# A mixed order for the heads, the rotary and the attention of a hybrid encoder on one core

## The reference

```python
proj = rmsnorm(h, norm_mix_even) @ w_in_ab            # z, x/B/C, dt, q, k, v: 24 tiles of 128 columns
# state space, 8 heads of 64, 2 groups, both directions
y = (d_skip[0] + d_skip[1]) * xs
for direction in range(2):
    dt = softplus(dt_raw + dt_bias[direction]);  A = -exp(a_log[direction])
    y = y + ssd_direction(xs, dt, A, bm, cm, reverse=(direction == 1))
ssd_out = rmsnorm_by_group(y * silu(z), norm_w)
# differential attention, 4 heads, two maps of 64 channels each, values of 128
q, k = partial_rotary(q), partial_rotary(k)
p = softmax(q @ k.T * 64 ** -0.5)
o = (p[:, :, 0] - lam * p[:, :, 1]) @ v
attn_out = rmsnorm(o, subln_w) * (1 - lambda_init)
h = h + concatenate([ssd_out, attn_out]) @ w_out_ab
h = h + swiglu(rmsnorm(h), w_gate, w_up, w_down)      # layer 0's second half
```

## Time and profile before

| what | us |
|---|---|
| median of 3 runs | 1687.55 |
| lowest and highest | 1683.24, 1688.83 |
| the profiled execution | 1691.67 |
| its span, first to last instruction | 1689.6 |
| its mean granted TensorE clock | 0.970 |

### The profile page before, as it was taken

One profiled execution on the slowest core, in us unless ns is written; L12 is line 12 of the kernel. 1 busy time (PEld: TensorE's weight loads), 2 busy tenths in 40 slices (PEclk: granted clock), 3 DMA queues, 4 the chain that ended last, 5 costly groups with the idle time before them and its releaser, 6 DMA issues.

```text
span 1689.6 us, 22187 instructions
## 1 busy us (share of the span) xinstructions
PE 1646.3 (97%) x8386; PEld 1365.2 (81%) x8390; DVE 1257.0 (74%) x1206; ACT 987.6 (58%) x905; POOL 65.1 (4%) x79
## 2 busy tenths in 40 slices
PE   8999899999999998999999999999999999999997
PEld 7766389999869667788888888888888888888886
DVE  5275766665456454788988988988988988988984
ACT  3363444443256412677777777776776777777673
POOL 0141000000100410000000000000000000000000
PEclk9989899999979897999999999999999999999998
DMA  8322035567305321899999999999999999999991
GB/s 273 100 75 75 1 100 175 174 202 221 100 17 167 116 85 65 300 373 342 355 372 340 359 368 342 358 367 344 357 368 346 352 371 342 356 371 343 354 370 74
DMA packets 221109, 429.55 MB, mean 254 GB/s; under 512 B 9506, under 2 KB 76584, under 8 KB 220736
## 3 DMA queue, kind: packets, MB, share of 16 engines
q1 hardware_dynamic: 217816, 424.82, 70.8%
q10 hardware_dynamic: 3240, 4.03, 0.7%
HBM read 427.77 MB, written 1.05 MB: 254 GB/s over the span
## 4 chain that ended last, share of the span: by engine, by line
PE 91%; DVE 4%; ACT 3%; issue 1%; DMA 1%; ACTq 0%; DVEq 0%
PE ps L1557 89%; PE ps L1574 3%; ACT arena L702 1%; DVE arena L999 0%; DVE ring_lo L1174 0%; DVE sq L1155 0%; ACT arena L601 0%; DMA raw<-in_moe_w_gate_dram 0%; DMA ktab<-in_k_table_dram 0%; DVE arena L1120 0%; ACT arena L845 0%; DVE arena L1284 0%; ACT arena L708 0%; DVE xn L1184 0%; ACT ring_hi L778 0%
## 5 line engine op out<-in xcount | busy, mean ns | idle before, releaser
L1345 DVE TENSOR_TENSOR w_lo<-raw,w_hi 128x2048 fp32r<-128x2048 f32 x224 | 511.5, 2290 | 73.7 <-ACT w_hi L890 72.6
L890 ACT ACTIVATE w_hi<-raw 128x2048 fp32r<-128x2048 f32 x224 | 429.1, 1919 | 169.1 <-DMA raw<-in_moe_w_gate_dram 87.7
L1557 PE MATMUL ps<-w_hi,xg_hi 128*128 128x512 f32 x904 | 358.5, 397 | 4.7 <-DVE w_lo L1525 2.1
L1557 PE MATMUL ps<-w_hi,xg_lo 128*128 128x512 f32 x904 | 353.0, 391 | 0.0
L1557 PE MATMUL ps<-w_lo,xg_hi 128*128 128x512 f32 x904 | 352.4, 390 | 0.0
L1349 DVE TENSOR_TENSOR w_lo<-raw,w_hi 128x2048 fp32r<-128x2048 f32 x110 | 251.6, 2287 | 48.8 <-ACT w_hi L894 48.6
L894 ACT ACTIVATE w_hi<-raw 128x2048 fp32r<-128x2048 f32 x110 | 211.1, 1919 | 86.4 <-DMA raw<-in_moe_w_down_dram 85.4
L1557 PEld LDWEIGHTS ps<-w_hi,xg_hi 128*128 128x128 f32 x904 | 170.2, 188 | 39.0 <-DVE w_lo L1525 2.5
L1557 PEld LDWEIGHTS ps<-w_hi,xg_lo 128*128 128x128 f32 x904 | 170.0, 188 | 36.4
L1557 PEld LDWEIGHTS ps<-w_lo,xg_hi 128*128 128x128 f32 x904 | 170.4, 189 | 33.5
L1557 PE MATMUL ps<-w_hi,eh_hi 128*128 128x512 f32 x440 | 172.8, 393 | 1.6 <-issue 1.6
(11 more groups left out here) (280 smaller groups left out, 1972.9 us busy)
## 6 DMA issues: line engine op xcount, KB each, us to landing
raw<-in_moe_w_gate_dram SPq DMA_DIRECT2D x112, 1024.0 KB, 5.0
raw<-in_moe_w_up_dram SPq DMA_DIRECT2D x112, 1024.0 KB, 5.1
raw<-in_moe_w_down_dram SPq DMA_DIRECT2D x112, 1024.0 KB, 5.0
ring<-in_w_in_ab_dram SPq DMA_DIRECT2D x12, 1024.0 KB, 6.5
ring<-in_hy_w_in_dram SPq DMA_DIRECT2D x12, 1024.0 KB, 5.1
ring<-in_ffn_w_gate_dram SPq DMA_DIRECT2D x11, 1024.0 KB, 5.3
ring<-in_ffn_w_up_dram SPq DMA_DIRECT2D x11, 1024.0 KB, 5.3
ring<-in_ffn_w_down_dram SPq DMA_DIRECT2D x8, 1408.0 KB, 7.5
```

What stands on the lines that cost most here:

```text
L890: nc.scalar.activation(w_hi[:, j, :], raw[:, j, :], ACT.Copy).then_inc(sem("gu_high"), 1)
L1345: V.tensor_tensor(w_lo[:, j, :], raw[:, j, :], w_hi[:, j, :].bitcast(F32), ALU.subtract).then_inc(sem("gu_split"), 1)
L1557: return nc.tensor.matmul(o, l, r, start=start, stop=stop)
```

## The change

- **Order.** The three filter layers follow projections 7, 9 and 11. Rotary products stand between projections 19, 20 and 21; the scores of heads 0 and 1 and the new tails come before projections 22 and 23. In attention each head's map is turned first, then the scores of head h + 2 are issued.
- **SSD.** DVE does `masks` and `decay_sums` for both heads of a step and then both `masked` products; `ssd_out(step - 2)` stands at the head of the step. `state_output` goes through the token tiles and interleaves the two heads. The second direction's cumulative sums lie on partitions 32 to 39, with a second copy of `sel8` there. All eight cosine products are on POOL, between its `W1` tiles.
- **Attention.** Only two token tiles of a head have scores of their own (4 tiles). The last 32 tokens of all four heads are put into two tiles `tail`, 32 partitions for each head, and combined once.
- **Norms.** Sums are taken with a narrow matrix `ind` (2 or 4 output rows, one for each group or head), roots and reciprocals are taken of these rows, and `spread` products bring them to all partitions (`nb`), which DVE reads from PSUM.
- **Zero products.** 40 in place of 68: 8 ahead of the first scores, 4 ahead of each head's turned map, 4 more ahead of the values of heads 2 and 3, 8 ahead of the first spread product.
- Later stages use `bank[...]` for `ps[...]`, a renumbering by the new length of the list. `harg` moves within the arena; the last sine goes to `fin`.

```diff
-    add("proj", 4, 8)
+    add("proj", 4, 4)
+    add("mlp", 0)
+    add("proj", 8, 2)
+    add("mlp", 1)
+    add("proj", 10, 2)
+    add("mlp", 2)
...
-    add("proj", 20, 2)
+    add("rope", 0, 4)
+    add("proj", 20)
+    add("rope", 4, 2)
     add("y", 3)
+    add("rope", 6, 2)
+    add("proj", 21)
+    add("score", 0, 4)
+    add("tail", 0, 2)
+    add("score", 4, 4)
     add("proj", 22, 2)
-    add("rope", 0, 8)
-    add("gss", 0, 2)
     add("vt", 0, 3)
-    add("score", 0, 6)
     for h in range(ATT):
-        if h + 1 < ATT:
-            add("score", 6 * h + 6, 6)
         add("at", 3 * h, 3)
+        if h + 2 < ATT:
+            add("score", 4 * h + 8, 4)
+        if h == 2:
+            add("ns", 0)
         add("o", h)
-    add("oss", 0, 4)
-    add("mlp", 0)
-    add("wo", 0, 4)
-    add("mlp", 1)
-    add("wo", 4, 4)
+    add("nb", 0, 2)
+    add("ns", 1)
+    add("nb", 2, 4)
+    add("wo", 0, 8)
...
         def _(pool):
             for h in range(HEADS):
                 pool.wait_ge(sem("dt_ready"), 1)
                 if h >= 2:
-                    pool.wait_ge(sem("m_ready"), h - 1)
+                    pool.wait_ge(sem("w1_used"), h - 1)
...
+                for j in ((), (), (), (0,), (1,), (2,), (3,), (4, 5, 6, 7))[h]:
+                    pool.wait_ge(used("proj"), 13 + j)
+                    g(nc.gpsimd.tensor_tensor(by_cos[:, j, :], qk[:, j, :], cosT, ALU.mult), sem("by_cos"))
...
         def _(act):
+            projected(20)
+            projected(21)
+            exps(0, 0)
+            exps(0, 1)
+            exps(None, 0)
+            exps(1, 0)
+            exps(1, 1)
+            projected(22)
+            projected(23)
+            for tt, (t0, n) in enumerate(TOKS):
+                copy("vt", tt, vT[0:n, tt, :], n, slice(0, 512))
+            turned_map(0)
             act.wait_ge(sem("yz_ready"), 4)
             a(nc.scalar.activation(sq[:, 0:4, :], ysb, ACT.Square), sem("act_squares"))
...
+            for h in (2, 3):
+                exps(h, 0)
+                exps(h, 1)
+                turned_map(h - 1)
+            t = ready(act, "ns", 0)
+            a(nc.scalar.activation(csr[0:2, 0, :], t[0:2, 0:T], ACT.Sqrt, bias=eps[0:2, 0:1], scale=1.0 / 256), used("ns"))
+            turned_map(3)
...
         def _(dve):
+            for step in range(4):
+                if step >= 2:
+                    ssd_out(step - 2)
+                for h in (2 * step, 2 * step + 1):
+                    masks(h)
+                    decay_sums(h)
+                masked(2 * step)
+                masked(2 * step + 1)
+            ssd_out(2)
             for j in range(8):
+                rotated(j)
+            ssd_out(3)
...
+            softmaxes(1)
+            softmaxes(2)
+            head_out(0)
+            softmaxes(3)
+            head_out(1)
+            head_out(2)
...
         def _(pe):
             def state_output(pair):
                 o = open_tile("y", pair)
-                for h in (2 * pair, 2 * pair + 1):
-                    pe.wait_ge(sem("m_ready"), h + 1)
-                    r = 64 * (h % 2)
-                    for tt, (t0, n) in enumerate(TOKS):
+
+                pe.wait_ge(sem("m_ready"), 2 * pair + 2)
+                for tt, (t0, n) in enumerate(TOKS):
+                    for h in (2 * pair, 2 * pair + 1):
+                        r = 64 * (h % 2)
                         last = mm(o[r:r + 64, 0:T], xT[0:n, tt, 64 * h:64 * h + 64], M[0:n, h % 4, tt, :], tt == 0, tt == 2)
+                close(last)
...
+            def tail_scores():
+
+                for m in range(2):
+                    o = open_tile("tail", m)
+                    r = slice(64 * m, 64 * m + 64)
+                    for h in range(ATT):
+                        last = mm(o[32 * h:32 * h + 32, 0:T], qk[r, h, T - 32:T], qk[r, 4 + h, :])
+                    close(last)
...
+            rotary(0, 4)
+            linear("proj", 20, 10, xn, which=(0,))
+            rotary(4, 2)
             state_output(3)
+            rotary(6, 2)
+            linear("proj", 20, 10, xn, which=(1,))
+            occupy(open_tile("score", 0), 8)
+            pe.wait_ge(sem("qk_ready"), 8)
+            scores(0)
+            tail_scores()
+            scores(1)
             linear("proj", 22, 11, xn)
...
             for h in range(ATT):
+                turn_map(h)
+                if h + 2 < ATT:
+                    scores(h + 2)
+                if h == 2:
+
+                    pe.wait_ge(sem("act_squares"), 1)
+                    o = open_tile("ns", 0)
+                    for q in range(4):
+                        last = mm(o[0:2, 0:T], ind[:, 3 - q // 2:5 - q // 2], sq[:, q, :], q == 0, q == 3)
                     close(last)
+                values(h)
```

More of the change, by code:

```diff
@@ L253, in trunk @@
         ps = [ctx.enter_context(nc.psum_tensor(f"ps{i}", [P, 512], F32)) for i in range(8)]
+        bank = [ps[(len(ORDER) + 2 + b) % 8] for b in range(8)]
         hT = sb("hT", [P, KT, T])
@@ L273, in trunk @@
         crd = sb("crd", [P, 16])
+        ind = sb("ind", [P, 8])
         zero16 = sb("zero16", [P, 512], BF16)
@@ L740, in _ @@
-            a(nc.scalar.activation(lam[:, 2:4], lam[:, 0:2], ACT.Exp), sem("lam_exp"))
[L742 to L749, removed]
-                        a(nc.scalar.activation(pr[0:n, (3 * h + tt) % 2, m, :], t[0:n, 0:T], ACT.Exp,
-                                               bias=stat[0:n, k, 0:1], accum_out=stat[0:n, k, 1:2]), used("score"))
@@ new lines, in head_max, with head_combine @@
+            def head_max(h, tt):
+                for m in range(2):
+                    k = 4 * h + 2 * tt + m
+                    row_max(k, ready(dve, "score", k))
+            def head_combine(h, tt):
+                k = 4 * h + 2 * tt
+                combine(2 * h + tt + (h > 0), (k, k + 1), at_[:, 2 * h + tt, :], (used("score"), k + 2))
+            head_max(0, 0)
+            head_max(0, 1)
+            head_combine(0, 0)
+            for m in range(2):
+                row_max(16 + m, ready(dve, "tail", m))
@@ new lines, in rotary, with scores @@
+            def rotary(first, n):
+                for j in range(first, first + n):
+                    pe.wait_ge(used("proj"), 13 + j)
+                    o = open_tile("rope", j)
+                    close(mm(o[:, 0:T], perm, qk[:, j, :]))
+            def scores(h):
+                for tt in range(2):
+                    for m in range(2):
+                        o = open_tile("score", 4 * h + 2 * tt + m)
+                        r = slice(64 * m, 64 * m + 64)
+                        close(mm(o[:, 0:T], qk[r, h, P * tt:P * tt + P], qk[r, 4 + h, :]))
@@ L1685, in state_output, with values @@
+            def values(h):
+                o = open_tile("o", h)
+                if h + 2 >= ATT:
+                    occupy(o, 4)
+                pe.wait_ge(used("at"), 3 * h + 3)
+                for kt, (k0, m) in enumerate(TOKS):
+                    last = mm(o[:, 0:T], vT[0:m, kt, P * h:P * h + P], aT[0:m, h % 2, kt, :], kt == 0, kt == 2)
                 close(last)
@@ new lines, in _ @@
+            occupy(open_tile("nb", 0), 8)
+            pe.wait_ge(sem("norm_rows"), 1)
+            for g in range(2):
+                spread(g, 2, g, 0)
+            o = open_tile("ns", 1)
+            for k in range(4):
+                pe.wait_ge(sem("act_squares"), 2 if k < 3 else 3)
+                last = mm(o[0:4, 0:T], ind[:, 3 - k:7 - k], sq[:, 4 + k, :], k == 0, k == 3)
+            close(last)
+            out_columns(0, 0)
+            out_columns(1, 0)
+            pe.wait_ge(sem("norm_rows"), 2)
@@ L1769, in _ @@
+            for k in range(4):
+                spread(2 + k, 4, k, 1)
+            out_columns(2, 0)
+            out_columns(3, 0)
+            for j in range(4):
+                out_columns(j, 1)
             add_squares("ss2", "squares2", 0, 2)
@@ L1969, in down @@
                         for half in range(2):
-                            last = product(ps[4 + half][:, :], rows[0][:, 2 * j + k, :], rows[1][:, 2 * j + k, :],
+                            last = product(bank[4 + half][:, :], rows[0][:, 2 * j + k, :], rows[1][:, 2 * j + k, :],
                                            [a[:, k, 512 * half:512 * half + 512] for a in w], begin and j + k == 0, end and j + k == 2)
```

403 lines of the change are left out of this document (185 added, 218 removed).

## The result

The changed kernel took 1663.88 us in the median (1660.06 to 1665.41, 4 runs), the kernel before 1688.19 in the same comparison: ratio 0.9858, 95% interval 0.9832 to 0.9884, faster by 24.3 us. The forecast was 1658, with 1650 to 1673. The profiled execution took 1660.06 us, its span is 1658.3.

What follows compares the result with a forecast made beforehand. DVE and ACT alternately held the chain until 118.7 us, then PE, with 10.2 us lost to half clock. Savings of 30.5 + 0.6 = 31.1, less 1.7 for one low stretch, net 29.4: 1687.55 to 1658, range 1650 to 1673.

Steps and rivals of the forecast that it cites:

- Filter layers: Layer 0, three filter layers moved ahead between projections: 1.9 us more on PE, decay rows at 82.55, relus at 83.4.
- SSD pairs: State space stage, heads in pairs: DVE never pauses, sets the pace at 11.6 us a step, and ends at 131.8.
- rival B: State outputs and tails: column groups don't overlap on PE, 5 to 7.5 us later, 1664; chance 0.18.
- Rotary in the gaps: Before attention: PE waits 3.8 us ahead of y(3); first scores start at 140.5 instead of 164.9.
- The two ends: Ahead of the first scores: PE's zero products end at 140.5, DVE's `rotated` at 140.4; either being late moves the start.
- Attention: Attention: PE sets the pace, its work sums to 40.7 us, output projection begins at 181.2 instead of 212.8.
- rival C: Attention drops to the lower clock with fewer zero products: two stretches make 1668, the whole at least 1674; chance 0.16.
- Output projection: Output projection: 32.3 us less a layer 0.6 and stall 0.2, plus spreads 1.9: 33.4, ending at 214.6.
- Clock: Layer 0: of 10.2 us lost, one 3.4 us stretch stays, costing 1.7, likeliest after the wait ahead of y(3).
- Rival E: Behind layer 0: nothing of the gain arrives because something there doesn't move with it, 1687; chance 0.02.
- D: From 82.6 to 214.6 us: 62 of 132 us at the lower clock undo the gain, all give 1722; chance 0.03.
- The rule on turns: Attention: transposes don't count as busy to the clock gate, so removing zero products beside them would lower the clock.

## Why the prediction was right, and where its sizes were off

The steps held, and their sum was 4.7 us too short at the feed-forward (214.6 against 219.31), or 3.0 with the 1.7 us that the forecast left for the clock. In the medians 24.3 us were saved where 29.4 were forecast. In the prediction's own order:

1. **Filter layers.** Taken: 1.9 us of PE, so decay rows at 82.55 and relus at 83.4. Measured: 81.33 and 82.14, which is 0.7 us later than before. DVE starts its first sums at 85.31, 1.2 us before the 86.5 assumed. DVE's and ACT's part was hidden, as said. That the 1.9 was too much is not shown, since the mark of the first decay row moves by more than 1.2 us from one profile to the next.
2. **SSD pairs.** DVE never pauses: right. Its last masked product ends at 133.6, not 131.8. The mis-sized term is POOL beside DVE: the work without it was 42.8 us, 48.3 were measured (85.31 to 133.60), so 5.5 us where 2.5 were taken. The upper bound of the prediction, 2.5 + 3.6, held. The 2.5 had been read from a stretch with POOL at `W1` alone, and for `W1` it was about right (2.2 by the rows). The eight cosine products were put at nothing within their bound of 3.6, and came to 3.2. Half of `W1` on ACT moved the end by 1.7, which confirms that part by experiment; the part of the cosine products rests on the rows that lie beside them. Overlap in columns, taken from a row of overlap in rows: 1.74 us against 1.7 taken; rival B is refuted by this row.
 Ahead of y(2) PE waits 1.87 us for the masked product. The prediction does not name this wait, but its pace of 11.6 us for DVE against 10.4 for PE implies it, and it costs nothing.
3. **Rotary in the gaps.** The wait ahead of y(3) was 2.23 us instead of 3.8, since the wait ahead of y(2), the lower clock after 123.0 and a wait of 0.48 had made PE later. From y(3) to the first scores 8.5 us against 8.1. Scores at 142.69 instead of 140.5: 1.8 of the 2.2 us are DVE's, from step 2. The two ends met within 0.5 us (last `rotated` at 142.2).
4. **Attention.** 41.64 us against 40.7; PE sets the pace. No rival C in this kernel: 1.00 in the whole window.
5. **Output projection.** 34.98 us against 33.4. The 1.6 is one stretch of low clock, 191.30 to 194.70, at half speed 1.7 us; without it, in the first run without zero products, the stage took 33.34.
 **Clock.** One short stretch was left for, two came. The one from 123.0 cost nothing on the path, because PE still waited 2.23 us for DVE after it. The one from 191.3 cost the 1.7 us that had been left. The size was thus right and the place wrong, which is luck. The place named, at the wait ahead of y(3), stayed at 1.00 here, but three variants fell right there for 6.8 us: both with `W1` on ACT, and the second without zero products.

In the profile, 1.2 us early, 3.0 late from contention, 0.4 between y(3) and the scores, 0.9 in attention and 1.6 in the output projection make the 4.7.

Rival E is refuted (25.8 us arrived at the feed-forward, and behind it no more than the spread is missing), D too. The prediction counted the zero products in full as PE's work. Taking them out showed that 5.4 of their 8.7 us are on the path. It kept C at 0.16 as the fate of a kernel with fewer zero products. With none, the old attention falls to the lower clock for 51.2 us, and the new one for 0, 3.4 and 10.2 us in three profiles (the last with `W1` on ACT as well); without them the new kernel gains all the same. The rule on turns quoted there stays undecided: with turns and no zero products the clock held at 1.00 for 36.57 us once, and fell in the two other profiles, with no wait of PE in attention above 1.3 us in any of them.

Where the gain comes from: undone one at a time, overlap costs 11 us, pairs 4 and order 9 by the ratios, each to within 6 or 7 us. In the profiles, at the feed-forward and counted from the first decay row, they cost 6.3, 6.5 and 11.3. Done alone in the kernel before, overlap gives 2.5 and pairs 1.9, both inside what can't be told from nothing. The traces say why: with the pairs alone PE's serial products set the pace, with the overlap alone DVE's waits for ACT do. The kernel before with both and nothing else was not run, so how much the two give together is not shown. The tails, the narrow norms and the place of the filter layers were not tried apart.

## What to carry to other kernels

When two engines release each other, try shortening both sides in one edit: each alone measured as nothing here, and each undone alone cost several us. A filler product earns its time by the waits that it fills. Taking all of them out cost 0.3% in the attention whose waits were then 2.0 to 4.7 us, and gained 0.3 to 0.5% in the one whose waits were then at most 1.3 us, although the clock fell there in two profiles of three. So try it again after each change that shortens waits. Compare marks from the start of the stage, and take a second profile before a cause is named: a saving of 8.1 us that looked like 8.7 us of fillers was 5.4 us of them and 2.7 us of luck. And when work is moved onto an idle engine, charge its neighbour: the price of a duration comes from rows with the same company.

## What the runs showed of the hardware

- Tiles of 32 columns and 64 rows overlap almost wholly. Sixteen records of the tails start between 143.5 and 144.1 and last 0.4 us each:

```profile
L1605 PE MATMUL ps<-arena x18: 389/389/413, 143.5 to 144.1; 64*32 64x272 f32 x16, 64*128 64x272 f32 x2
```

 So both tiles of the tails started within some 0.6 us, where the prediction took 1.0 for them.
- POOL's own time varies too: a cosine product is 1.11 us at 106.22, beside DVE's masked products, and 0.76 at 126.66, where DVE's masks beside it took 2.10 us instead of 1.56.
- The clock fell without any wait: in the changed kernel without overlap, and in the kernel before with pairs alone, PE has no idle time from the first decay row to the falls at 104 and 118 us. State outputs of 64 columns and decay rows of 8 rows stood right ahead. In the changed kernel, where both overlap, one stretch of 3.4 us was left ahead of the scores, and it came after a wait of 1.87 us.
- The sine stands among `Silu` activations (line 703) without a table load. Between 56 and 222 us loads of 1.28 us come only with the exponential (88.33) and the root (172.19):

```profile
62.51 0.44 ACT L698 ACTIVATE arena<-arena 64x288 f32<-64x288 f32 x1 [2.89 <-DVE arena L1099]
88.33 1.28 ACT L733 ACT_TABLE_LOAD   x1
```

- The same program draws other stretches of the lower clock in other executions (211.5 and 216.4 at the feed-forward), so a profile's marks carry up to some 5 us of luck, and a verdict on less needs the medians.
